# WKV stage: corner blocks of the chunk inverses made at once, one inverse product a step from the fifth step on, and a new order of the products behind it

## The chip, the cores and the metric

The kernel runs on one core of a Trainium2 chip (trn2). The metric is the device time of one execution in microseconds (us): median of 3 runs 2166.91, from 2166.88 to 2168.07. The profiler's execution has a span of 2162.8 us, 4.1 us less than that median; a number below is a number of that execution.

## The reference, cut to what matters

Two model blocks over 256 tokens of width 2048: attention, pooling and a gated feed-forward block, then an RWKV-7 mixer and a differential-attention mixer, all in fp32. The change lies in the mixer's recurrence:

```python
def step(S, inp):                       # 32 heads of 64 channels, 256 tokens
    r_t, w_t, k_t, v_t, kk_t, a_t = inp
    sa = jnp.einsum('bhvk,bhk->bhv', S, kk_t)
    S = (S * w_t[:, :, None, :]
         - sa[..., None] * (kk_t * a_t)[:, :, None, :]
         + v_t[..., None] * k_t[:, :, None, :])
    y = jnp.einsum('bhvk,bhk->bhv', S, r_t)
    return S, y
```

Behind it every head's output is normalised (group norm), scaled, a bonus term is added, it is gated by silu(g) and multiplied by `w_out`.

## The kernel before, in words

The heads are taken as 4 groups g of 8 heads, the tokens as 4 chunks c of 64 (`CHUNK`, `NCH`), which gives 16 steps n = 4g + c (`STEPS`). Inside a chunk the recurrence is solved by products of matrices: u = T x, where T is the inverse of a 64 x 64 unit-triangular matrix of each head and chunk. State S is carried from chunk to chunk of one group.

Ahead of the steps, beside 96 woven units of a projection, VectorE (DVE) inverts only the two 32 x 32 diagonal blocks of every T (`inverse_step`, L2983; `LT`, `TT`), 128 head-chunk pairs at once. They go to DRAM (`t_scratch`, L729) and come back step by step in the places that the products want (`load_t`, L665: four transfers of the diagonal blocks, two of the off-diagonal block `CRS` of the matrix itself). The corner of T is never made: a step multiplies by the diagonal blocks (u), by the corner of the matrix (w), adds w to x and multiplies by the diagonal blocks again.

One step on TensorE (PE; `step`, L1458) in program order, each product 8 calls of `quads` (L1313, one line L1319 for all) or 4 calls of a turn, and every fp32 call two matmul instructions in the trace: `x_second` (kappa by S), `k_pairs` of step n+1, first u product, `turn_v` of n+1, w product, (in the first step of a later group `group_squares` of the group before), `beta_pairs` of n+1, first part of y (r by S), second u product, `turn_k` of n+1, state product, `turn_beta` of n+1, `x_first` of n+1, second part of y. Turns of k and beta are left out where step n+1 is the last of its group (c = 3), the state product where n is.

Beside it ScalarE (ACT; `step`, L2231) copies x (L2234), the y of the step before (L2205), u (L2240), the turned v (L2210), half of the second u (L2246), the turned k and beta (L2216). DVE (`step`, L3051) masks the pairs (`read_kappa` L3037, `read_rho` L3043), adds w (L3057), copies the other half of the second u (L3063), adds to S and scales it (L3075, L3077). At some steps both do what belongs elsewhere: DVE a reciprocal at c = 0 of g = 1, 2, 3 (`head_reciprocal`), a `head_pair` at steps 7, 9, 11, 13, low halves of output weights (L2448) at steps 10, 14, 15, 15 (`LOW_SPLIT_AT`); ACT their high halves (L1692) at steps 6, 10, 14, 14 (`SPLIT_AT`). GpSimd (POOL) squares y (L866). SyncE (SP) issues every transfer, in program order, with its waits. Behind step 15 the output product starts as soon as the first four tiles of its operand are split (`operand_hi`, `operand_lo`, L2229, L3049).

The order is written by hand on every engine; no planner changes it.

## Time and profile before

| what | number |
|---|---|
| median of 3 runs | 2166.91 us |
| span of the profiled execution | 2162.8 us |
| PE busy | 2128.1 us (98%) |
| DVE, ACT busy | 1466.9, 1063.6 us (68%, 49%) |
| granted TensorE clock | full (2.4 GHz) in all 40 slices |
| instruction transfers (q8) | 88 of 1.44 MB in all, so 16 KB each |

A timeline row gives the start in us, the length, the engine, the line, the operation with what it writes and reads, and how many instructions are merged in it; a bracket is the engine's idle time before it and who ended it. PE's matmuls are pipelined, so the distance from one row's start to the next is what a product costs, not its length.

### The profile page before, as it was taken

The page shows a single profiled execution, that of the slowest core. Times are in us where ns is not written, and L with a number is a line of the kernel's source. Part 1 is how long each engine was busy: PE and PEld are TensorE (multiplying, and loading weights), DVE is VectorE, ACT ScalarE, POOL GpSimd, SP SyncE. Part 2 cuts the span into 40 slices and gives each one's busy share as a digit, 9 for nine tenths or more (in the row PEclk, how much of TensorE's full clock was granted, in tenths as well). Part 3 has the DMA queues.
Part 4 walks back from the last instruction along what each step waited for, and adds up shares of the span by engine and source line. Part 5 has one row for each costly group of instructions (what it writes and reads, how often), then busy time and mean ns, then how long its engine had stood idle before and what let it go on. Part 6 is the DMA issues. An engine that isn't in the chain of part 4 may idle for free.

```text
span 2162.8 us, 36139 instructions
## 1 busy us (share of the span) xinstructions
PE 2128.1 (98%) x13990; PEld 1808.1 (84%) x13990; DVE 1466.9 (68%) x2083; ACT 1063.6 (49%) x1516; POOL 85.8 (4%) x75
## 2 busy tenths in 40 slices
PE   9999999999999999999899999999899999999998
PEld 7888878888888888888788888887788888888886
DVE  6556568885478855786795599884776544567656
ACT  5444455444444433444644766544434534456543
POOL 0800000000000000000000000001211000000000
PEclk9999999999999999999999999999999999999999
DMA  9654545555656556555465656653454555654553
GB/s 299 202 165 157 172 160 185 190 186 189 198 185 190 187 187 199 187 180 177 150 203 167 196 183 179 206 160 86 129 174 142 185 185 195 186 155 146 173 197 117
DMA packets 398856, 384.43 MB, mean 178 GB/s; under 512 B 43660, under 2 KB 395460, under 8 KB 397764
## 3 DMA queue, kind: packets, MB, share of 16 engines
q1 hardware_dynamic: 398728, 382.66, 55.8%
q8 instruction: 88, 1.44, 0.3%
q14 instruction: 40, 0.33, 0.1%
HBM read 375.73 MB, written 6.87 MB: 177 GB/s over the span
## 4 chain that ended last, share of the span: by engine, by line
PE 89%; DVE 7%; issue 2%; ACT 1%; DMA 1%; POOL 0%; SPq 0%; DVEq 0%; ACTq 0%; POOLq 0%
PE acc L894 35%; PE acc L897 17%; PE acc L1020 5%; PE acc L1022 5%; PE acc L1021 5%; PE acc L931 3%; PE acc L986 2%; PE acc L987 2%; PE acc L988 2%; PE aux L1319 2%; PE acc L934 1%; DVE w_lo L3001 1%; PE acc L1619 1%; PE acc L1620 1%; PE acc L1621 1%
## 5 line engine op out<-in xcount | busy, mean ns | idle before, releaser
L2448 DVE TENSOR_TENSOR w_lo<-raw_w,w_hi 128x1024 fp32r<-128x1024 f32 (+1 forms) x570 | 683.5, 1224 | 438.3 <-ACT w_hi L1692 437.5
L1692 ACT ACTIVATE w_hi<-raw_w 128x1024 fp32r<-128x1024 f32 (+1 forms) x570 | 586.3, 1045 | 706.0 <-PE acc L897 413.0
L894 PE MATMUL acc<-h,w_hi 128*128 128x512 f32 x1664 | 525.8, 397 | 0.0
L897 PEld LDWEIGHTS acc<-h,w_lo 128*128 128x128 f32 x1664 | 312.6, 188 | 73.8
L897 PE MATMUL acc<-h,w_lo 128*128 128x256 f32 x1664 | 327.0, 278 | 0.0
L894 PEld LDWEIGHTS acc<-h,w_hi 128*128 128x128 f32 x1664 | 254.7, 189 | 1.0
L894 PE MATMUL acc<-x_split,w_hi 128*128 128x512 f32 x704 | 225.1, 401 | 0.0
L894 PE MATMUL acc<-xs_b,w_hi 128*128 128x512 f32 x512 | 162.0, 398 | 1.0 <-DVE w_lo L3001 0.9
L897 PEld LDWEIGHTS acc<-x_split,w_lo 128*128 128x128 f32 x704 | 132.2, 188 | 31.2
L3001 DVE TENSOR_TENSOR w_lo<-raw_w,w_hi 128x1024 fp32r<-128x1024 f32 x96 | 116.8, 1219 | 42.1 <-ACT w_hi L2165 41.2
L894 PE MATMUL acc<-xs_a,w_hi 128*128 128x512 f32 x448 | 142.3, 399 | 0.7 <-DVE w_lo L3001 0.7
L897 PE MATMUL acc<-x_split,w_lo 128*128 128x256 f32 x704 | 138.7, 278 | 0.0
L1020 PE MATMUL acc<-w_hi,ff 128*128 128x512 f32 x346 | 135.2, 391 | 2.9 <-DVE w_lo L2448 2.9
L1021 PE MATMUL acc<-w_lo,ff 128*128 128x512 f32 x352 | 137.5, 391 | 0.0
L1022 PE MATMUL acc<-w_hi,ff 128*128 128x512 f32 x346 | 135.1, 390 | 0.0
L2165 ACT ACTIVATE w_hi<-raw_w 128x1024 fp32r<-128x1024 f32 x96 | 100.8, 1054 | 53.2 <-PE acc L897 45.6
L897 PEld LDWEIGHTS acc<-xs_b,w_lo 128*128 128x128 f32 x512 | 96.2, 188 | 22.7
L894 PEld LDWEIGHTS acc<-x_split,w_hi 128*128 128x128 f32 x704 | 108.1, 189 | 2.4 <-issue 0.8
L897 PEld LDWEIGHTS acc<-xs_a,w_lo 128*128 128x128 f32 x448 | 84.2, 188 | 20.0
L897 PE MATMUL acc<-xs_b,w_lo 128*128 128x256 f32 x512 | 100.6, 278 | 0.0
L897 PE MATMUL acc<-xs_a,w_lo 128*128 128x256 f32 x448 | 88.1, 278 | 0.0
L894 PEld LDWEIGHTS acc<-xs_b,w_hi 128*128 128x128 f32 x512 | 78.0, 189 | 3.4 <-issue 1.6
(459 smaller groups left out, 3223.5 us busy)
## 6 DMA issues: line engine op xcount, KB each, us to landing
raw_w<-in_w_up SPq DMA_DIRECT2D x172, 512.0 KB, 3.5
raw_w<-in_a_w_in SPq DMA_DIRECT2D x124, 512.0 KB, 3.9
raw_w<-in_w_in SPq DMA_DIRECT2D x64, 512.0 KB, 3.9
raw_w<-in_w_down SPq DMA_DIRECT2D x64, 512.0 KB, 3.5
raw_w<-in_b_w_qg SPq DMA_DIRECT2D x64, 512.0 KB, 3.7
raw_w<-in_w_o SPq DMA_DIRECT2D x32, 512.0 KB, 3.5
raw_w<-in_a_w_out SPq DMA_DIRECT2D x32, 512.0 KB, 3.5
raw_w<-in_w_k_shared SPq DMA_DIRECT2D x32, 512.0 KB, 3.3
```

Of the source, the lines that this page charges most:

```text
L894: pe.matmul(ACC[2 * b + f], WHI[:, q if hi is None else hi, k, f * P:(f + 1) * P], op[:, kt, :, :].rearrange("p h t -> p (h t)"), start=fi ...
L897: mm = pe.matmul(ACC[2 * b + f][:, 0:T], WLO[:, slot, k, f * P:(f + 1) * P], op[:, kt, 0, :], start=False, stop=last)
L931: pe.matmul(ACC[2 * b + f], hi(2 * x + b)[:, k, f * P:(f + 1) * P], op[:, kt, :, :].rearrange("p h t -> p (h t)"), start=first, stop=False)
L986: pe.matmul(out, xh, wh[:, :, k, :], start=(kt == 0), stop=False)
L987: pe.matmul(out, xh, wl[:, :, k, :], start=False, stop=False)
L1020: pe.matmul(out[t_], xh, wh, start=(x + k == 0), stop=False)
L1021: pe.matmul(out[t_], xh, wl, start=False, stop=False)
L1022: mm = pe.matmul(out[t_], xl, wh, start=False, stop=(x == 3 and k == ku - 1))
L1692: act.activation(WHI[:, u % 4, 0:ku, :], RAWW[:, u, 0:ku, :], ACT.Copy).then_inc(hi_made, 1)
L2165: act.activation(WHI[:, n % 4, :, :], RAWW[:, slot, :, :], ACT.Copy).then_inc(hi_made, 1)
L2448: dve.tensor_tensor(WLO[:, u, 0:ku, :], RAWW[:, u, 0:ku, :], WHI[:, u % 4, 0:ku, :].bitcast(F32), ALU.subtract)\
L3001: dve.tensor_tensor(WLO[:, slot_of(n), :, :], RAWW[:, slot_of(n), :, :], WHI[:, n % 4, :, :].bitcast(F32), ALU.subtract)\
```

## The change

The corners of all T are now made once. TT's blocks are stored in whole 64 x 64 places of `t_scratch` whose corners are blanked first (`blank_corners`). ACT writes the first diagonal blocks turned (`left_turned`), they go out and come back by row (`LEFT_ALL`), the second diagonal blocks come back too (`RIGHT_ALL`), the matrices' corners are loaded at once (`CROSS_ALL`). PE makes corner products of 128 calls of 32 x 32 by 32 in step 0 and again in step 1; ACT and DVE copy their results, and SP stores the corners of groups 1 to 3. Steps 0 to 3 (`WHOLE` = 4) still use two u products and w. From step 4 on `whole_step` uses the whole T: one u product, and right behind it the state product; the turns of v, k and beta, `k_pairs` (now two steps ahead) and `x_first` follow. The first part of y stands ahead of u, the group's squares at the end of the step, y has one PSUM bank in turn, S two buffers. ACT and DVE follow that order; `read_kappa` looks two steps ahead and stands ahead of the reciprocal, the head pairs and the splits. `load_t` is one transfer from step 4 on. The bonus rows are spread behind the stored corners. The diff, without declarations of buffers and semaphores, and without lines taken away from functions printed above:

```diff
@@ -561,8 +569,32 @@
...
-STATE_SUMS = BANKS[:, 3, T:].rearrange("p (e x) -> p e x", e=2)
-XU_BANKS, Y_BANKS = SIDE[:, 0:2, :], SIDE[:, 2:4, :]
+GROUP_SUMS = BANKS[:, 3, T:]
+XU_BANKS, CORNER_BANKS = SIDE[:, 0:2, :], SIDE[:, 2:4, :]
+WHOLE = NCH
+CORNERS_IN, CORNERS_COPIED, ALL_STORED = 16 + 12 * 16, 2, 5 * 16
+def y_bank(n):
+    return SIDE[:, 2 + n % 2, 0:T].rearrange("p (e x) -> p e x", e=2)
+def state_sums(n):
+    return SIDE[:, 2 + (n + 1) % 2, T:].rearrange("p (e x) -> p e x", e=2)
+def s_after(n):
+    return (S, S_ODD)[n % NCH % 2]
+def u_count(n):
+    return n + 1 + min(n + 1, WHOLE)
+def us_count(n):
+    return 2 * (n + 1) + min(n + 1, WHOLE)
+def t_count(n):
+    return sum(16 if k >= WHOLE else 48 for k in range(n % 3, n + 1, 3))
@@ -665,14 +697,29 @@
 def load_t(n):
...
-    src = t_dram.rearrange("(f c h) b s t -> c h b s f t", c=NCH, h=2)
-    for hh in range(2):
-        for b in range(2):
-            at = 64 * hh + H * b
-            sp.dma_start(TB[at:at + H, m, :, H * b:H * b + H], src[c, hh, b, :, 4 * g:4 * g + 4, :])\
-              .then_inc(t_loaded[m], 16)
-    for e in range(2):
-        sp.dma_start(CRS[64 * (1 - e):64 * (1 - e) + H, m, :, H:], cross_dram[g, c, e]).then_inc(t_loaded[m], 16)
+    src = t_dram.rearrange("(g i c h) s t -> g c (h s) i t", g=4, c=NCH, h=2)
+    sp.dma_start(TB[:, m, :, :], src[g, c]).then_inc(t_loaded[m], 16)
+    if n < WHOLE:
+        for e in range(2):
+            sp.dma_start(CRS[64 * (1 - e):64 * (1 - e) + H, m, :, H:], cross_dram[g, c, e]).then_inc(t_loaded[m], 16)
+def blank_corners():
+    sp.wait_ge(blanked, 2)
+    for a, b in ((0, H), (H, 0)):
+        sp.dma_start(t_dram[:, a:a + H, b:b + H], TB[:, 0, 0:1, 0:H].broadcast_to([P, H, H])).then_inc(t_stored, 16)
+def load_left_and_right(g):
+    sp.dma_start(LEFT_ALL[H * g:H * g + H, :, :], left_dram[32 * g:32 * g + 32].rearrange("a r s -> r a s")).then_inc(inv_in, 16)
+    sp.dma_start(RIGHT_ALL[H * g:H * g + H, :, :], t_dram[32 * g:32 * g + 32, H:, H:].rearrange("a s t -> s a t")).then_inc(inv_in, 16)
+def store_corners():
+    sp.wait_ge(blanked, 2 + 2 * CORNERS_COPIED)
+    for g in range(1, 4):
+        sp.dma_start(t_dram[32 * g:32 * g + 32, 0:H, H:].rearrange("a s t -> s a t"), CORNERS[H * g:H * g + H, :, :])\
+          .then_inc(bon_stored, 16)
 def store_lt(f):
@@ -724,13 +771,22 @@
...
+    if n == 88:
+        blank_corners()
...
-sp.dma_start(t_dram, TT[:, :, :, :]).then_inc(t_stored, 16)
-sp.wait_ge(blanked, 2)
-sp.wait_ge(t_stored, 16)
-for n in range(3):
-    load_t(n)
+for b in range(2):
+    sp.dma_start(t_dram[:, H * b:H * b + H, H * b:H * b + H], TT[:, b, :, :]).then_inc(t_stored, 16)
+for g in range(4):
+    sp.dma_start(CROSS_ALL[H * g:H * g + H, :, :].rearrange("s (b x) t -> s b (x t)", x=4), cross_dram[g].rearrange("c e s x t -> s (c e) (x t)")).then_inc(inv_in, 16)
+sp.wait_ge(inverted, 2)
+sp.dma_start(left_dram, OUTER[:, :].rearrange("p (r s) -> p r s", r=H)).then_inc(t_stored, 16)
+sp.wait_ge(t_stored, ALL_STORED)
+load_t(0)
+for g in range(4):
+    load_left_and_right(g)
+load_t(1)
+load_t(2)
 def first_unit(n, w):
@@ -757,11 +813,15 @@
...
-for g in range(4):
-    spread_bonus(g)
...
+    if n == WHOLE:
+        sp.wait_ge(bon_stored, 64 + 48)
...
+    if n == WHOLE - 1:
+        store_corners()
+        for g in range(4):
+            spread_bonus(g)
@@ -1453,52 +1513,120 @@
     g, c = STEPS[n]
     pe.wait_ge(x_begun, 3 * g + c)
     pe.wait_ge(s_ready, 3 * g + c)
...
+    quads(XU_BANKS, 0, at(KAP, n), state(n), between, False, True).then_inc(x_done, 1)
+def u_product(n):
+    quads(XU_BANKS, P, block_of(TB[:, n % 3, :, :]), mid(XS), across, True, True).then_inc(u_done, 1)
+def state_product(n):
+    g, c = STEPS[n]
+    pe.wait_ge(us_ready, us_count(n))
+    if c < 3:
+        pe.wait_ge(kb_out, k_beta_turned(n))
+        pe.wait_ge(y_out, n)
+        quads(state_sums(n), 0, kb(n % 2), vu(n % 2), channel, True, True, one_bank=True).then_inc(s_done, 1)
+def y_first(n):
+    if n > 1:
+        pe.wait_ge(y_out, n - 1)
+    quads(y_bank(n), 0, state(n), at(R, n), channel, True, False, one_bank=True)
+def y_second(n):
+    pe.wait_ge(rest_out, n + 1)
+    if n > 1:
+        pe.wait_ge(y_out, n - 1)
+    quads(y_bank(n), 0, vu(n % 2), rho(n % 2), channel, n % NCH == 0, True, one_bank=True).then_inc(y_done, 1)
+def corner_products(lhs, rhs):
+    for a in range(H):
+        for g in range(4):
+            rows = slice(H * g, H * g + H)
+            mm = pe.matmul(CORNER_BANKS[rows, a // 16, a % 16 * H:a % 16 * H + H], lhs(a)[rows], rhs[rows, a, :], start=True, stop=True)
+    mm.then_inc(corner_done, 1)
+def cross_of(a):
+    i, c, hh = a // 8, a // 2 % 4, a % 2
+    return CROSS_ALL[:, 8 * c + i % 2 * 4 + 2 * (hh ^ i % 2) + i // 2, :]
+def corners_halfway():
+    pe.wait_ge(inv_in, CORNERS_IN)
+    pe.wait_ge(kb_out, 1)
+    corner_products(cross_of, LEFT_ALL)
+def corners():
+    pe.wait_ge(blanked, 2 + CORNERS_COPIED)
+    pe.wait_ge(y_out, 1)
+    corner_products(lambda a: HALFWAY[:, a, :], RIGHT_ALL)
 def step(n):
     g, c = STEPS[n]
...
+    state_next = STEPS[n + 1][1] < 3
+    if c > 0:
+        x_second(n)
+    k_pairs(n + 1)
+    pe.wait_ge(t_loaded[n % 3], t_count(n))
+    pe.wait_ge(xs_ready, n + 1)
+    u_product(n)
+    turn_v(n + 1)
+    pe.wait_ge(us_ready, us_count(n) - 2)
+    quads(XU_BANKS, T, far(CRS[:, n % 3, :, :]), far(US), between, True, True).then_inc(w_done, 1)
+    if n == 0:
+        corners_halfway()
+    if n == 1:
+        corners()
+    beta_pairs(n + 1)
+    if n > 1:
+        y_first(n)
+    pe.wait_ge(ws_ready, n + 1)
+    u_product(n)
+    if state_next:
+        turn_k(n + 1)
+    if n < 2:
+        pe.wait_ge(blanked, 2 + CORNERS_COPIED * (n + 1))
+    if n == 1:
+        y_first(n)
+    state_product(n)
+    if state_next:
+        turn_beta(n + 1)
+    if n + 1 < WHOLE:
+        x_first(n + 1)
+    y_second(n)
+    if n + 1 == WHOLE:
+        k_pairs(n + 2)
+        x_first(n + 1)
+def whole_step(n):
+    g, c = STEPS[n]
     more = n + 1 < len(STEPS)
     state_next = more and STEPS[n + 1][1] < 3
...
     if c > 0:
         x_second(n)
+        y_first(n)
     if more:
...
+        beta_pairs(n + 1)
+    pe.wait_ge(t_loaded[n % 3], t_count(n))
     pe.wait_ge(xs_ready, n + 1)
...
+    u_product(n)
+    state_product(n)
+    if c == 2:
+        pe.wait_ge(gn_read, g)
     if more:
         turn_v(n + 1)
...
+    y_second(n)
     if state_next:
         turn_k(n + 1)
...
     if state_next:
         turn_beta(n + 1)
...
+    if c == 0:
+        pe.wait_ge(vt_out, 2 * n + 4)
+        group_squares(g - 1)
+    if n + 2 < len(STEPS):
+        k_pairs(n + 2)
+    if more:
         x_first(n + 1)
...
 gates = [quarters(operand, per) for per in (1, 2, 2)]
 for n in range(NW):
@@ -2145,6 +2276,11 @@
 def pair_hi(s_, p):
...
+def left_turned():
+    act.wait_ge(inverted, 1)
+    act.activation(OUTER[:, :].rearrange("p (r s) -> p r s", r=H), TT[:, 0, :, :].rearrange("p s r -> p r s"), ACT.Copy).then_inc(inverted, 1)
 def woven_out(j0):
@@ -2202,7 +2340,12 @@
...
+    act.activation(y4, by_two(y_bank(n)), ACT.Copy).then_inc(y_out, 1)
+def corner_copy(n):
+    act.wait_ge(corner_done, n + 1)
+    act.activation((HALFWAY, CORNERS)[n][:, 0:H // 2, :], CORNER_BANKS[:, 0, :].rearrange("p (a t) -> p a t", a=H // 2), ACT.Copy).then_inc(blanked, 1)
 def v_copies(n):
@@ -2230,23 +2373,32 @@
 def step(n):
     g, c = STEPS[n]
+    more = n + 1 < len(STEPS)
     act.wait_ge(x_done, n + 1)
     act.activation(in_slots(XS), by_two(XU_BANKS[:, :, 0:P]), ACT.Copy).then_inc(xs_ready, 1)
...
+    if n < WHOLE:
+        if n:
+            y_copy(n - 1)
+        else:
+            woven_out(2)
+        act.wait_ge(u_done, u_count(n) - 1)
+        act.activation(in_slots(US), by_two(XU_BANKS[:, :, P:T]), ACT.Copy).then_inc(us_ready, 1)
         v_copies(n + 1)
...
+        if n < 2:
+            corner_copy(n)
+    act.wait_ge(u_done, u_count(n))
     act.activation(v_and_u(n % 2)[0:64, :, 1, :, :].rearrange("p j h t -> p h j t"), by_two(XU_BANKS[0:64, :, P:T]), ACT.Copy)\
        .then_inc(us_ready, 1)
...
+    if n >= WHOLE and more:
+        v_copies(n + 1)
+    elif n >= WHOLE:
+        operand_hi(0)
+    if n >= WHOLE and more:
+        y_copy(n)
+    if more:
         k_beta_copy(n + 1)
+    if n == WHOLE - 1:
+        y_copy(n)
     if n == 0:
         silu(7)
     if n == 2:
@@ -3051,15 +3203,14 @@
 def step(n):
     g, c = STEPS[n]
     more = n + 1 < len(STEPS)
...
+    if n < WHOLE:
         read_kappa(n + 1)
...
+        dve.wait_ge(w_done, n + 1)
+        dve.tensor_tensor(slots(XS), by_two(XU_BANKS[:, :, T:384]), slots(XS), ALU.add).then_inc(ws_ready, 1)
+    if n < 2:
+        dve.wait_ge(corner_done, n + 1)
+        dve.tensor_copy((HALFWAY, CORNERS)[n][:, H // 2:, :], CORNER_BANKS[:, 1, :].rearrange("p (a t) -> p a t", a=H // 2)).then_inc(blanked, 1)
+    dve.wait_ge(u_done, u_count(n))
     dve.tensor_copy(v_and_u(n % 2)[64:P, :, 0, :, :].rearrange("p j h t -> p h j t"), by_two(XU_BANKS[64:P, :, P:T])).then_inc(us_ready, 1)
     if more:
         read_rho(n + 1)
@@ -3068,28 +3219,29 @@
     if c < 3:
         decay = GCE[:, 4 * g:4 * g + 4, c].rearrange("p (j e) -> p e j", e=2).unsqueeze(3).broadcast_to([P, 2, 2, CHUNK])
+        s_new, ps = slots(s_after(n)), by_two(state_sums(n))
         dve.wait_ge(s_done, 3 * g + c + 1)
...
         if c > 0:
...
+            dve.tensor_tensor(s_new, ps, slots(s_after(n - 1)), ALU.add).then_inc(s_taken, 1)
+            dve.wait_ge(s_taken, 2 * g + c)
+            dve.tensor_tensor(s_new, s_new, decay, ALU.mult).then_inc(s_ready, 1)
         else:
...
+            dve.tensor_tensor(s_new, ps, decay, ALU.mult).then_inc(s_ready, 1)
+    pair = 2 * (g - 2) + 1 if c == 1 and g > 1 else 2 * (g - 1) if c == 3 and 0 < g < 3 else None
+    wide = [GWIDE[:, (2 if c == 1 else 0) + k, :] for k in range(2)]
+    if c == 0 and g:
+        dve.wait_ge(gn_sq_sum, g)
+        dve.tensor_scalar(GROWS[:, 0, :], GROUP_SUMS, 1.0 / CHUNK, GN_EPS, ALU.mult, ALU.add).then_inc(gn_read, 1)
+    if n + 1 >= WHOLE and n + 2 < len(STEPS):
+        read_kappa(n + 2)
     if c == 0 and g:
         head_reciprocal(g - 1)
...
     for u in heads_at(n, LOW_SPLIT_AT):
         split_unit(u)
...
+    if pair is not None:
+        if c == 3:
+            dve.wait_ge(gn_loaded, 32 * g)
+        head_pair(pair, wide)
 def head_reciprocal(g):
     dve.wait_ge(gn_read, g + 1)
```

## Rows read from the trace of the kernel before

**Rows 1.** Stretches: busy us and instructions by engine, clock, DMA share, GB/s.
```profile
1448.50:1458.40 9.90, 9.90 (x59) 8.63 (x57) 4.28 (x4) 3.32 (x5) 0.00 (x0) 1.00 0.18 28
1467.30:1563.90 96.60, 86.59 (x2666) 70.87 (x2665) 55.83 (x109) 48.41 (x117) 23.50 (x24) 1.00 0.34 90
```
**Rows 2.** Timeline, PE: second u product of step 3; the output product's first.
```profile
1488.59 0.46 PE L1319 MATMUL aux<-wkv_x,inverse_blocks 64*64 64x64 f32 x16
...
1563.88 0.74 PE L931 MATMUL acc<-wkv_out,w_hi 128*128 128x512 f32 x2 [0.57 <-DVE wkv_out L3049]
```
**Rows 3.** Timeline of PE alone, step 9, from turn_v to step 10's x.
```profile
1523.78 0.66 PE L1401 MATMUL acc<-consts,x 128*64 128x128 f32 x8
1524.37 0.46 PE L1319 MATMUL aux<-wkv_u,cross_blocks 64*64 64x64 f32 x16
1524.65 0.41 PE L1386 MATMUL acc<-r_kappa,beta 64*64 64x64 f32 x16
...
1525.38 0.46 PE L1319 MATMUL aux<-wkv_x,inverse_blocks 64*64 64x64 f32 x16
1525.77 0.66 PE L1407 MATMUL acc<-consts,k 128*64 128x128 f32 x8
1526.39 0.69 PE L1319 MATMUL acc<-wkv_small 128*64 128x64 f32 x16
1526.90 0.61 PE L1407 MATMUL acc<-consts,beta 128*64 128x128 f32 x8
1527.44 1.08 PE L1319 MATMUL aux<-wkv_small 64*64 64x64 f32 x32
1528.45 0.46 PE L1319 MATMUL aux<-wkv_s,r_kappa 64*64 64x64 f32 x16
```
**Rows 4.** Timeline of all engines, step 10's second u to step 11's first.
```profile
1531.49 0.46 PE L1319 MATMUL aux<-wkv_x,inverse_blocks 64*64 64x64 f32 x16
...
1532.02 0.43 DVE L3063 COPY wkv_small<-aux 64x256 f32<-64x256 f32 x1 [0.58 <-PE aux L1319]
...
1532.51 0.69 PE L1319 MATMUL acc<-wkv_small 128*64 128x64 f32 x16 [0.55 <-DVE wkv_small L3063]
...
1534.31 0.46 PE L1319 MATMUL aux<-wkv_s,r_kappa 64*64 64x64 f32 x16
1534.56 0.65 PE L1376 MATMUL acc<-r_kappa,k 64*64 64x128 f32 x16
...
1534.83 0.38 ACT L2234 ACTIVATE wkv_x<-aux 128x256 f32<-128x256 f32 x1 [1.48 <-PE aux L1319]
...
1535.28 0.42 DVE L3037 TENSOR_TENSOR wkv_small<-acc,consts 128x256 f32<-128x256 f32 x1
...
1535.36 0.46 PE L1319 MATMUL aux<-wkv_x,inverse_blocks 64*64 64x64 f32 x16
```
**Rows 5.** Timeline: side work of DVE and ACT, group squares on PE.
```profile
1527.92 0.87 DVE L3108 SCALAR_TENSOR_TENSOR beta<-beta,params,head_rstd_wide 128x256 f32<-128x256 f32 x2
...
1528.83 0.88 DVE L3113 SCALAR_TENSOR_TENSOR beta<-beta,params,bonus 128x256 f32<-128x256 f32 x2
...
1542.70 0.64 PE L1423 MATMUL aux<-group_norm_squares,consts 128*32 128x128 f32 x16 [0.79 <-POOL group_norm_squares L866]
...
1545.82 1.75 DVE L3096 RECIPROCAL head_rstd_rows<-head_rstd_rows 128x256 f32<-128x256 f32 x1
...
1556.55 1.99 ACT L1692 ACTIVATE w_hi<-raw_w 128x1024 fp32r<-128x1024 f32 x2
...
1562.60 1.23 DVE L3049 TENSOR_TENSOR wkv_out<-beta,wkv_out 128x1024 fp32r<-128x1024 f32 x1
```
**Rows 6.** Timeline of SP: the inverses' store and the first load back.
```profile
1442.55 0.34 SPq L729 DMA_DIRECT2D t_scratch<-inverse  x1
1448.43 1.76 SPq L672 DMA_DIRECT2D inverse_blocks<-t_scratch  x4
```
**Rows 7.** Timeline, step 5: a product broken in its middle.
```profile
1501.05 0.32 PEld L1319 LDWEIGHTS aux<-wkv_x,inverse_blocks 64*64 64x64 f32 x15 [0.91 <-issue]
```

More of the change, by code:

```diff
@@ L275, in program @@
                 with ExitStack() as s3:
+                    CORNERS = sb(s3, "corners", [P, CHUNK // 2, CHUNK // 2])
+                with ExitStack() as s3:
                     HTP = sb(s3, "xs_pair", [P, 2, T])
@@ L303, in program @@
                     LT, TT = (sb(s3, n, [P, 2, CHUNK // 2, CHUNK // 2]) for n in ("lt_blocks", "inverse"))
+                with ExitStack() as s3:
+                    CROSS_ALL, LEFT_ALL, RIGHT_ALL, HALFWAY = (sb(s3, n, [P, CHUNK // 2, CHUNK // 2])
+                                                               for n in ("cross_all", "left_all", "right_all", "corner_halfway"))
                 BON = sb(s2, "bonus", [P, KD, T])
@@ L1422, in group_squares @@
                     for i in range(4):
[L1423 removed]
+                        mm = pe.matmul(GROUP_SUMS[32 * i:32 * i + 32, e * P:(e + 1) * P], HEADSEL[:, 30:62], GSQ[:, i, e * P:(e + 1) * P], start=True, stop=True)
                 mm.then_inc(gn_sq_sum, 1)
```

90 lines of the change are left out of this document (16 added, 74 removed).

## The prediction

> **What bounds the kernel now.** I read the page first: TensorE is busy nearly all the span at full clock, so outside the changed stage nothing can move but through PE. Then the stretches [rows 1]: the sixteen steps last from about 1467.3 to 1563.9, and in these 96.6 us PE has 86.6 us in work, DVE 55.8 and ACT 48.4. So the stage is mostly a queue of small products on PE, with some waiting. Then the timeline of one step [rows 3] against one with a shorter queue [rows 4]: from one product's start to the next there is no hole in the first, while in the second PE stands 0.55 us in front of the state product, waiting for DVE's copy of u. That is what decides this change: in the old order a turn of k fills the time in which u is copied, in the new order the state product is directly behind u and nothing fills it.
>
> **Prices from these rows.** A 64x64 product whose four tiles work together (x's second term, w) costs 0.25 to 0.28; u about 0.39 with its entry [rows 3, 4]. The state product costs 0.51. x's first and y's second term together take 1.01 [rows 3]; x takes 0.25 and y is of the state product's kind, 0.51, so 0.25 is left for two changes of the tile shape, 0.12 each. Turn of beta 0.54, less one change 0.42; turn_v 0.59, less a change and its slower entry 0.43; turn of k taken as 0.43. k_pairs: its row is 0.65 long where x's row is 0.46 for a cost of 0.25, so 0.65 - 0.21 = 0.44 [rows 4]. Latencies [rows 4]: u's start to the state product's 1.02 (copy begins at 0.53); state product to the next x term at least 1.80; x term to u 1.05 (copy begins at 0.52); k_pairs to the mask of kappa 0.72, which lasts 0.42.
>
> **Whole steps (4 to 15).** Behind the start S of the state product PE now has: state 0.51, turn_v 0.43, y 0.51, turn_k 0.43, turn_beta 0.42, one change 0.12, k_pairs 0.44, x_first 0.25, in all 3.11. That is over the 1.80 that the state itself needs, so PE's queue sets it. Then x to u 1.05, which hides y's first term and beta_pairs (0.25 + 0.73 [rows 3] = 0.98), and u to S 1.02, of which 0.6 is bare. A step with c = 1 costs 3.11 + 1.05 + 1.02 = 5.18. c = 2 has no turns of k and beta, 5.18 - 0.85 = 4.33. c = 3 has no state product and x_first stands in x_second's place, 5.18 - 0.51 - 0.25 = 4.42. c = 0 has the group squares as well, whose row is like a turn's [rows 5], with a change on either side about 0.5: 5.68; the 0.79 that they waited for POOL goes, since the squares of the group before are then a whole step old.
> From step 3's second u product [rows 2] to step 4's u: 1.02 to us's arrival, turn_beta 0.42, y 0.51, change 0.12, k_pairs 0.44, x to u 1.05 = 3.56. Three c = 0 steps 17.04, three c = 1 15.54, two c = 2 8.66, two c = 3 8.84. Step 14: 1.02 + 1.80 + 1.05 = 3.87. Step 15 to the output product: ACT's copy ends at 0.91, only then comes its high half (1.0, half of the row of two in [rows 5], the same shape), then DVE's low half 1.23, so 3.3. Sum 60.8.
> **What the side work costs.** It was behind PE's queue and is now in front of a copy that PE waits for. The mask of kappa ends 1.14 behind k_pairs' start; the reciprocal adds 1.75, in all 2.89 [rows 5]. The next u copy is wanted at 0.44 + 0.25 + 1.05 + 0.53 = 2.27: 0.6 late, three times, 1.9. A head pair is 0.87 + 0.04 + 0.88 = 1.79: 0.66 late at steps 9 and 13, and at 7 and 11, where no x_second lies between, 0.91 late: 3.1. ACT's split (1.0) stands between y's copy, which ends about 3.3 behind u, and the next x copy, wanted at 3.8 in steps 6 and 10: 0.57 late twice, 1.1; in step 14 there are two, ready at 5.35 against 3.34: 2.0. Together 8.1, so 60.8 + 8.1 = 68.9. The old stretch is 1563.88 - 1488.59 = 75.3 [rows 2]. **Gain 6.4 us.** Its bounds: 8.1 more if none of the side work comes in the way, and 3 us less if each of the 12 steps keeps a change of tile shape and a longer entry of 0.25.
>
> **Steps 0 and 1: the corner products.** Nothing goes out of these steps, and each gets 128 calls, 256 matmuls. Neither 32x32 tiles nor 32 columns at this rate occur in the trace. Sixteen instructions of 64x64 by 64 take 0.25. If columns bound, half of it per sixteen: 16 x 0.125 = 2.0 us a product. If issue bounds, 16 x 0.25 = 4.0. There is a third price: loads and matmuls together are 512 instructions, while the whole stage issues 5331 in 96.6 us, 55 per us [rows 1]; in 2 us that would be 250 per us. That code arrives late even at the low rate is my reading of step 5, where one product stands 0.91 after its first weight load with "issue" as the cause, so with no semaphore to wait for [rows 7]; two such holes a product give 2.0 + 1.8 = 3.8, and with issue as bound 5.8. I take 3.4, nearer to the middle of the first two, because some code is already there, and keep 2.0 and 5.8. Behind the product DVE and ACT copy 512 columns before the copy of u; turn_k hides most in step 0 (0.1 left with the change of shape), and in step 1 turn_k and the moved y term do, at 0.1 to 0.3. Sum 2 x 3.4 + 0.2 = **7.0 us lost.**
>
> The page TensorEngine Tiling of the Trainium skill, under Gotcha 1: PSUM Pressure, speaks against this change: row tiles cannot use the same PSUM bank at once. The corner products do this with four. In [rows 3] two row tiles write each bank in other partitions (x's term) at four tiles' full rate, so the trace does not agree for two. As a mechanism, tiles taken one after another would make 16 instructions cost 4 x 0.125 = 0.5 and a product 8.0.
> TensorE: Matmul & The Clock Gate of the same skill, under Wait — 56ns, not 53.3ns?, gives about 25 ns as the least distance between matmul starts; 256 of them would be 6.4 us a product and the whole 2174.0 by that page, an estimate. The row has 16 in 0.25 us, 16 ns each [rows 4], so it does not hold across tiles here.
>
> **Transfers.** SP stored the inverses at 1442.55 and could load at 1448.43 [rows 6]. Now in that place: two stores of 4096 pieces of 128 bytes, four loads of corners, a wait for ACT's turned block (free at about 1448), its store. Between 1448.5 and 1458.4 eighteen loads with 128 pieces each took 0.18 of 16 engines [rows 1], 28.5 engine-us for 2304 pieces, 12.4 ns a piece: two stores are 6.3 us. Stored at about 1457.5, step 0's T in at about 1460, well before step 0 (1467.3). The eight loads of left and right blocks, 1024 pieces each, are 6.3 us more: in at about 1467.5 with their latency, wanted in front of the first corner product at about 1469.7. Hidden, with 2 us to spare; if that cover goes, each piece that takes twice as long costs up to 10 us. I put 0.5 us into the sum. The blanking, 6.3 us of DMA time beside weights, meets loads asked for some 7 units ahead. Later loads get shorter (one instead of six) and the bonus rows are spread later but needed only at step 7: nothing.
>
> **Sum.** -6.4 + 7.0 + 0.5 = +1.1: span 2163.9, and with the 4.1 us between this execution and the median **2168.0 us**.
>
> **Rivals.**
> 1. Faster. DVE's and ACT's side work fits into gaps (say half of the 8.1 is not felt) and columns bound the corner products: gain 10.4, cost 4.2, 2166.9 - 6.2 = 2160.7. For it: DVE is busy only 58% of the stage [rows 1]. Against it: the order on each engine is fixed, and the reciprocal stands right there.
> 2. Slower: step 0 waits for the left and right blocks. Price: if pieces of 128 bytes in long transfers need 18 instead of 12.4 ns, the stores end 3 us later and the loads another 3; less the 2 us of slack that is 4 us, and with code as the corner products' bound (3.8) one more: 2173. It decides from the point at which they land after 1469.7.
> 3. Slower still: the four tiles of a corner product work one after another (8.0 each): 2168.0 + 9.2 = 2177.
> 4. The corner products cost 2 us each and the rest is as forecast: 2165.2, within my forecast's own range.
>
> **Chances.** Forecast with its own range 2163 to 2172, 0.50 (rival 4 in it); faster 0.25; late loads or late code 0.20; serial tiles 0.05. This kernel's time can be told apart from no change at about 0.2%, 4.3 us: faster is below 2162.6, slower above 2171.2. Faster 0.25, within 0.49, slower 0.26. The range that leaves out two in ten reaches from 2160.5 (rival 1) to 2175 (most of rival 2).
>
> **What would show it.** Right: whole steps of 5.2, 4.3, 4.4 us and 5.7 for c = 0; a hole of about 0.6 us in front of every state product behind a u copy; the reciprocal, head pairs and splits followed by u or x copies that begin late; corner products of 2 to 4 us in steps 0 and 1; the output product 3.3 us behind the last u. Wrong: corner products over 5 us, or a wait for left_all or right_all in front of the first of them (rival 2 or 3); steps under 5 us at c = 0 and 1, with DVE free when u is ready (rival 1); PE holes with "issue" inside the corner products put the fault on code, not on tiles. The forecast is also wrong if weights of the woven units come late behind the blanking, which would show as PE waits around 1430 to 1445.

## The result, and the profile after

The changed kernel takes 2182.04 us (median of 4 runs, 2178.71 to 2187.66) against 2166.89 for the kernel before: ratio 1.0078, 95% interval 1.0061 to 1.0095. On a second chip it was 1.0073 (1.0056 to 1.0090). It is 15 us slower. The forecast was 2168.0 with a range from 2160.5 to 2175.0, so it was wrong by 14 us and outside its range.

The profiled execution took 2187.66 us (span 2186.1), the slowest of its four; its 23.3 us over the span before are placed first, and what is peculiar to it is named. These are the stretches of the changed kernel: steps 0 to 3 (from the first u product to step 3's second u product), the rest of the steps up to the output product's first matmul, the output product, and what follows. Columns: stretch and its length, busy us of PE, its weight loads, DVE, ACT and POOL with instructions, granted clock, DMA share, GB/s.

```profile
1466.18:1508.06 41.88, 29.46 (x1112) 24.88 (x1104) 10.86 (x22) 12.28 (x29) 1.84 (x3) 0.84 0.41 89
1508.06:1581.25 73.19, 56.86 (x1677) 50.31 (x1673) 43.08 (x77) 34.48 (x78) 22.82 (x21) 0.95 0.37 102
1581.25:1681.50 100.25, 98.56 (x583) 82.18 (x584) 69.46 (x78) 38.62 (x41) 7.59 (x5) 0.97 0.55 177
1681.50:2186.10 504.60, 495.69 (x2618) 421.08 (x2616) 296.78 (x380) 245.43 (x353) 5.43 (x4) 0.98 0.53 167
```

The same four stretches of the kernel before (cut at the same instructions; [rows 2] has two of the marks):

```profile
1467.80:1488.59 20.79, 18.65 (x600) 15.35 (x592) 9.47 (x20) 11.07 (x27) 1.84 (x3) 1.00 0.22 51
1488.59:1563.88 75.29, 67.42 (x2062) 55.01 (x2058) 46.34 (x89) 36.93 (x90) 21.64 (x21) 1.00 0.37 100
1563.88:1661.70 97.82, 95.95 (x583) 80.03 (x584) 69.43 (x78) 39.31 (x42) 8.73 (x5) 1.00 0.55 179
1661.70:2162.80 501.10, 494.14 (x2618) 419.73 (x2617) 296.64 (x380) 245.36 (x353) 5.44 (x4) 0.99 0.53 168
```

Line by line: steps 0 to 3 +21.1 us, steps 4 to 15 -2.1, output product +2.4, the rest +3.5, and the first u product begins 1.6 earlier (in the profiled runs below it begins anywhere from 1462.6 to 1468.9, except where calls are added ahead of it, so that is no effect of the change). Sum 23.3. In the last two stretches PE has the same number of instructions and less clock. The corner products of step 0, on PE (start, length, operation, what it stood idle for):

```profile
1467.92 0.46 PE L1379 MATMUL aux<-wkv_u,cross_blocks 64*64 64x64 f32 x16
1468.32 1.30 PE L1546 MATMUL aux<-left_all,cross_all 32*32 32x32 f32 x130
1471.37 1.27 PE L1546 MATMUL aux<-left_all,cross_all 32*32 32x32 f32 x126 [1.75 <-issue]
1472.57 0.32 PE L1446 MATMUL acc<-r_kappa,beta 64*64 64x64 f32 x2
1475.11 0.59 PE L1446 MATMUL acc<-r_kappa,beta 64*64 64x64 f32 x11 [2.21 <-issue]
```

The 256 matmuls run at 10 ns each, 2.57 us together, in two bursts, and behind each burst PE waits for nothing that has a semaphore. Between the two waits lie 126 + 2 = 128 matmuls with a weight load each: 256 instructions. In step 1 the same calls stand around waits of 1.1 and 2.5 us, again 128 matmuls apart. The waits of PE in steps 0 to 3 (engine and line, what ended the wait; us in total, times, longest):

```profile
PE aux L1546 <- issue: 5.3, 3, 2.5
PE aux L1379 <- issue: 3.1, 1, 3.1
PE acc L1446 <- issue: 2.2, 1, 2.2
PE acc L1461 <- DVE silu_g L2678: 0.7, 1, 0.7
PE aux L1379 <- DVE wkv_small L3214: 0.6, 1, 0.6
```

Issue waits are 10.6 us, the calls themselves 5.1. At a granted clock of 0.84, 13.4 of the 41.9 us ran at 1.2 GHz and not 2.4 (0.16 x 2 x 41.9). Of the 21.1 us by which these steps grew, 5.4 are left for that. One of its spells:

```profile
1474.40:1481.20 6.80, 6.09 (x114) 5.41 (x118) 1.54 (x3) 1.49 (x3) 0.00 (x0) 0.50 0.01 2
```

The 3.1 us wait stands in step 3's w product, far from any corner product; SP had just issued the spread of the bonus rows (SP's queue, then PE):

```profile
1492.70 5.56 SPq L800 DMA_DIRECT2D bonus<-bonus_scratch  x8
```

```profile
1507.08 0.40 PE L1379 MATMUL aux<-wkv_u,cross_blocks 64*64 64x64 f32 x12 [3.08 <-issue]
```

In step 9 DVE's head pair, whose first two instructions take 0.87 us in [rows 5], took long, while POOL multiplied the bonus rows. DVE's and POOL's timelines:

```profile
1545.84 2.57 DVE L3260 SCALAR_TENSOR_TENSOR beta<-beta,params,head_rstd_wide 128x256 f32<-128x256 f32 x2
```

```profile
1545.38 2.36 POOL L909 TENSOR_TENSOR bonus<-bonus,x 128x1024 f32<-128x1024 f32 x1
```

One of the two took 2.18 us and the other 0.47.

The trace also has the transfers that bring instructions (queue q8, 16384 bytes each). Each of the five issue waits in steps 0 to 3 ends shortly behind one of them:

| wait, us | it ends at | q8's transfer | wait's end behind it |
|---|---|---|---|
| 1.75 | 1471.37 | 1468.98 to 1470.07 | 1.30 |
| 2.21 | 1475.11 | 1472.48 to 1473.63 | 1.48 |
| 1.08 | 1485.30 | 1482.92 to 1483.88 | 1.42 |
| 2.46 | 1489.04 | 1486.46 to 1487.68 | 1.36 |
| 3.08 | 1507.08 | 1504.30 to 1505.55 | 1.53 |

The same holds for every issue wait of 0.8 us or more from 1455 to 1590 us in all seventeen profiled runs (55 waits): it ends 1.2 to 1.7 us behind a transfer that took 0.9 to 1.5 us. So these are waits for instructions.

What was feared did not come: with the blanking's transfers PE's stretch ahead of the steps is full at full clock, and no wait for the left and right blocks stands ahead of the corner product.

```profile
1430.00:1466.00 36.00, 36.00 (x271) 30.90 (x274) 20.98 (x30) 14.85 (x19) 0.00 (x0) 1.00 0.89 198
```

### The profile page after: what moved, and what is told of

Its sections match the earlier page's. It is cut to its first block, busy times and chain, and to the rows that moved or that the text cites. A ratio compares the mean times of both kernels' runs of the same rounds, so it can differ in the third digit from the quotient of the medians.

```text
span 2186.1 us, 36327 instructions
## 1 busy us (share of the span) xinstructions
PE 2131.7 (98%) x14118; PEld 1815.8 (83%) x14118; DVE 1465.4 (67%) x2073; ACT 1063.7 (49%) x1507; POOL 85.9 (4%) x75
## 4 chain that ended last, share of the span: by engine, by line
PE 90%; DVE 7%; issue 2%; ACT 1%; POOL 0%; DVEq 0%; ACTq 0%; POOLq 0%
PE acc L954 35%; PE acc L957 17%; PE acc L1080 5%; PE acc L1082 5%; PE acc L1081 5%; PE acc L991 3%; PE acc L1046 2%; PE acc L1047 2%; PE acc L1048 2%; PE acc L994 2%; PE aux L1379 2%; DVE w_lo L3153 1%; PE acc L1750 1%; PE acc L1751 1%; PE acc L1752 1%
```

## The experiments

Theory ("code"): TensorE's instructions come in pieces of 256. While small products run at 100 matmuls (200 instructions) per us, the next piece is not there yet, and each piece costs a wait of 1.3 to 2.7 us (1.1 to 2.7 in all runs); half clock follows the waits. Rivals: the small tiles or their columns are dear in themselves; the new order of the steps is the loss. Ratios are to the kernel before on the same chip.

**The same calls in the kernel before.**

```diff
+                if n < 2:
+                    for a in range(32):
+                        for q in range(4):
+                            rows = slice(32 * q, 32 * q + 32)
+                            pe.matmul(Y_BANKS[rows, 0, P:P + 32], IDENT[rows, 32 * q:32 * q + 32], CENTRE[rows, 0:32], start=True, stop=True)
                 if more:
                     beta_pairs(n + 1)
```

> The kernel before with 128 calls of 32 rows by 32 columns added in step 0 and in step 1, behind w, whose sums nobody reads; nothing is left out. Code theory: the same holes at every 256th instruction as in the changed kernel, 1.3 to 2.7 us each, and half clock behind some: 2167 + 9 to + 15 = 2176 to 2182. Rival (the calls cost only their columns, and the loss is in the new order): 2 x 2.0 to 2.5, so 2171 to 2172.

Measured: 2178.00 us, ratio 1.0071 (1.0054 to 1.0088), +14.2 us.

```profile
1462.64:1500.25 37.61, 27.96 (x1113) 24.16 (x1105) 9.48 (x20) 11.07 (x27) 1.84 (x3) 0.82 0.14 32
1500.25:1574.48 74.23, 67.63 (x2062) 55.21 (x2057) 46.38 (x89) 36.93 (x90) 21.62 (x21) 1.00 0.38 101
```

```profile
1464.77 1.30 PE L1481 MATMUL aux<-consts 32*32 32x32 f32 x130
1467.54 1.26 PE L1481 MATMUL aux<-consts 32*32 32x32 f32 x126 [1.46 <-issue]
1468.73 0.33 PE L1386 MATMUL acc<-r_kappa,beta 64*64 64x64 f32 x2
1471.55 0.59 PE L1386 MATMUL acc<-r_kappa,beta 64*64 64x64 f32 x12 [2.50 <-issue]
```

Without one transfer, copy or reordering of the change, steps 0 to 3 grow from 20.8 to 37.6 us, and the waits stand at the same places, 126 + 2 matmuls apart. Steps 4 to 15 give 1.1 us back. The time was inside the expected 2176 to 2182, and the whole loss can come from these calls. The DMA share there is 0.14, so no traffic is needed for it.

**A quarter of the columns.** The same edit with `P:P + 8` and `CENTRE[rows, 0:8]`.

> The kernel before with the 128 calls in step 0 and in step 1 again, now with 8 columns each in place of 32: the same number of instructions, a quarter of the columns. Nothing is left out. Code theory: the holes stay, 1.6 to 2.7 us at every 256th instruction; +11 to +15 over the kernel before. Rival (columns): +4 at most. The run with 32 columns was +14.

Measured: 2179.96 us, ratio 1.0071 (1.0055 to 1.0088), the same as with 32 columns.

```profile
1466.85 1.26 PE L1481 MATMUL aux<-consts 32*32 32x8 f32 x130
1469.81 1.22 PE L1481 MATMUL aux<-consts 32*32 32x8 f32 x126 [1.70 <-issue]
1470.96 0.32 PE L1386 MATMUL acc<-r_kappa,beta 64*64 64x64 f32 x2
1473.27 0.59 PE L1386 MATMUL acc<-r_kappa,beta 64*64 64x64 f32 x12 [1.99 <-issue]
```

Even the bursts last as long: columns cost nothing here, instructions do. The rival of columns falls.

In the seven profiled runs with all 128 calls together, the second wait of each product ends 3.46 to 4.01 us behind the first, 256 instructions later. That is the pace at which code came: the next transfer began 1.0 us or more after a wait's end, took about 1.1, and the wait ended about 1.4 behind it. A burst that uses up a piece in 1.3 us waits for the rest.

**The same calls beside wide matmuls.** The 256 calls of 32 columns, 32 behind each of eight units of the woven products (units 84 to 91).

> The kernel before with the same 256 calls (32 rows, 32 columns), but 32 behind each of eight units of the woven products, at about 1410 to 1445, where wide matmuls leave time for the code to come. Nothing is left out. Code theory: no holes, only their issue at 10 ns each: +5 to +6.5 us. Rival (the calls are dear wherever they stand): +14.

Measured: 2170.88 us, ratio 1.0027 (1.0016 to 1.0038), +5.7 us. The groups stand from 1431.7 to 1458.1, 3.67 us apart. The stretch that holds nearly all of them; the kernel before has x185 matmuls in the same stretch:

```profile
1430.00:1460.00 30.00, 30.00 (x645) 25.76 (x644) 19.52 (x28) 10.50 (x12) 0.00 (x0) 1.00 0.39 122
```

No wait of any kind and full clock. PE took 1289 instructions in these 30 us, 43 per us, under the 64 to 74 per us of the pace above; the expected 5 to 6.5 us came. So small calls are dear only where the instructions around them are short too.

**In portions.** The same 256 calls in eight portions of 32, two in each of steps 0 to 3 (ahead of y's first term and ahead of turn_k).

> The kernel before with the same 256 calls (32 rows, 32 columns) in eight portions of 32, two in each of steps 0 to 3. Nothing is left out. If the pace of the code decides (a piece of 256 instructions every 3.5 to 3.7 us, as the steps with corner products show): steps 0 to 3 have 2512 instructions, 9.8 pieces, 34 to 36 us against 20.8, so +13 to +15, or +10 if no half clock comes with it. Rival (only closeness is dear, and portions are hidden as beside the wide matmuls): +5 to +6.

Measured: 2174.97 us, ratio 1.0055 (1.0038 to 1.0071), +11.3 us. That lies between the two numbers for the pace (10 without half clock, 13 to 15 with it) and well over the rival's 5 to 6.

```profile
1464.60:1495.96 31.36, 25.47 (x1053) 21.74 (x1048) 9.48 (x20) 11.07 (x27) 1.84 (x3) 0.95 0.15 35
```

```profile
PE acc L1462 <- issue: 2.4, 2, 1.7
PE aux L1319 <- issue: 1.8, 2, 1.3
...
PE aux L1462 <- issue: 0.3, 1, 0.3
```

Seven of the eight portions lie in this stretch; the last stands behind the second u product of step 3. It grew by 10.6 us, of them 4.5 the calls and 4.5 issue waits. With steps 4 to 15 (76.4 us) that is 11.7 us, against 15.8 with the calls in two blocks: portions save some 4 us and hide little of the rest. The forecast's 2512 instructions were a wrong count: the stretch has 2101 (x1053 matmuls and x1048 loads), 8.2 pieces, 3.8 us a piece, within the 3.46 to 4.01 above. Without the calls it is 4.5 us a piece (x600 and x592 in 20.8 us) and there is no wait: these steps stood close to that pace already.

**The changed kernel with fewer instructions.** First 2 calls of 128 rows and 512 columns for each corner product, then 32 calls of 128 rows and 32 columns. Both leave out the correct corner blocks; all else is as it is. The first edit:

```diff
-                        rows = slice(H * g, H * g + H)
-                        mm = pe.matmul(CORNER_BANKS[rows, a // 16, a % 16 * H:a % 16 * H + H], lhs(a)[rows], rhs[rows, a, :], start=True, stop=True)
+                wide = (HALFWAY if rhs is RIGHT_ALL else CROSS_ALL).rearrange("p (a b) t -> p a (b t)", b=4)
+                for b in range(2):
+                    mm = pe.matmul(CORNER_BANKS[:, b, :], wide[:, b, :], rhs[:, 16 * b:16 * b + 16, :].rearrange("p a t -> p (a t)"), start=True, stop=True)
```

> The changed kernel with each corner product as 2 calls of 128 rows and 512 columns: eight instructions a product, about the same columns per bank, everything else as it is. The corner blocks and the output are wrong. Code theory: the four holes (8.3 us), the issue of the calls (some 4.4 us) and the half-clock spells (2 to 5 us) go, about 1 us of columns stays: 2182 - 14 to - 17 = 2165 to 2168. Rival (the new order of the steps is the loss, steps 0 to 3 included): not under 2176. My recorded forecast without its corner term would give 2161 to 2162.

> The changed kernel with each corner product as 32 calls of all 128 rows in place of 128 calls of 32 rows: the same columns go through, with a quarter of the instructions. The blocks beside the diagonal are left in, so the corner blocks and the output are wrong. Code theory (TensorE waits for its instructions, which come in pieces of 256): 768 instructions less are three pieces less; the holes of 1.94, 2.43, 1.27 and 2.65 us shrink to one at most, and the spells at half clock behind them with them: 2182 - 7 to - 12 = 2170 to 2175. Rival (columns or the tiles themselves are slow): the same time as the changed kernel, 2180 to 2182. Rival (the new order of the steps is the loss): also 2180 to 2182.

Measured: 2170.98 us, ratio 1.0034 (1.0022 to 1.0047) with 2 calls; 2191.10 us, ratio 1.0122 (1.0098 to 1.0147) with 32 (three runs; a fourth took 7012.71 us, unexplained). The first:

```profile
1464.10:1488.64 24.54, 22.64 (x608) 16.82 (x600) 10.86 (x22) 12.28 (x29) 1.84 (x3) 1.00 0.53 110
1488.64:1565.55 76.91, 56.64 (x1679) 49.90 (x1675) 43.08 (x77) 34.36 (x78) 22.85 (x21) 0.95 0.43 113
```

```profile
1466.24 1.98 PE L1545 MATMUL aux<-left_all,cross_all 128*128 128x512 f32 x4
...
1495.09 0.28 PE L1379 MATMUL aux<-wkv_small 64*64 64x64 f32 x4 [3.57 <-issue]
```

Steps 0 to 3 last 24.5 us: 3.8 over the kernel before. Each wide product takes 1.9 us and makes its step 1.6 longer (from first to second u product 4.33 us for 2.75, and 3.56 for 1.99), which is 3.2. So the new order itself costs these steps 0.6 us, and as the cause of the loss there that rival falls. But the whole is 3 to 6 us over what I expected: a wait of 3.6 for a piece of code still stands behind the bonus spread, which makes steps 4 to 15 76.9 us long. The 32-call kernel missed by 20 us, for a reason of its own:

```profile
1467.80 12.23 PEld L1545 LDWEIGHTS aux<-left_all,cross_all 128*128 128x128 f32 x64
```

Each call now loads 128 columns of weights for 32 columns of data, 191 ns a load, so packing four blocks on a diagonal is no way out. The clock was 0.57 there, and 0.50 from 1471 to 1480, with PE busy all the time and no wait. So waits are not needed for half clock: how much of it in the changed kernel goes back to them, and how much to the small calls themselves, is not shown. The Trainium skill states (TensorE: Matmul & The Clock Gate, "LDWEIGHTS (loading the stationary operand)") that a load's time goes by its columns, not by its rows. The trace of the kernel before agrees: loads of 64 columns took 134 ns with 64 rows and 136 with 128, loads of 128 columns 188 ns with 97 rows and with 128.

**Three groups of corner blocks.** Steps 0 to 3 never read the blocks of group 0, so `range(4)` became `range(1, 4)`.

> The changed kernel with the corner blocks of groups 1 to 3 alone (96 calls a product, not 128): steps 0 to 3 use the old corner path, so those of group 0 are never read. Nothing that is needed is left out. Code theory: 256 instructions less are one piece of code and one hole of about 2.4 us less and 1.3 us less of issue, with less half clock: 3 to 5 us under the changed kernel. Columns alone (rival): 1.3 us under it.

Beside it ran the changed kernel again:

> The changed kernel as it is, for a time on the same chip as the runs beside it: 1.007 to 1.009 of the kernel before.

Measured: 2177.74 us against 2181.41, ratios 1.0056 (1.0040 to 1.0073) and 1.0073 (1.0056 to 1.0090): 3.7 us less, of which 1.3 is issue, as the code theory expected (3 to 5 us). The two intervals overlap; the stretch tells more: steps 0 to 3 took 35.15 us in place of 40.17.

**The bonus spread later.** Two broadcasts each in steps 4 to 7, GpSimd's products at steps 5, 7, 9, 11.

> The changed kernel with the spread of the bonus rows (eight broadcasts) taken from step 3 and given as two each to steps 4 to 7, with GpSimd's product of them two steps later. Nothing is left out. Code theory: the hole of 3.3 us in step 3's w product was a piece of code that stood behind the spread; it shrinks to 0 to 1 us, with some 1 us of half clock behind it: 2182 - 3 to - 4.5 = 2177.5 to 2179. Moving GpSimd's product also moves its collision with VectorE's head pair in step 9 (2.18 us for an instruction of 0.48). Rival (that hole is only the pace at which code comes after the corner products): within 1 us of 2182.

Measured: 2179.81 us, ratio 1.0075 (1.0058 to 1.0091).

```profile
1464.88:1502.94 38.06, 28.61 (x1113) 24.20 (x1105) 10.85 (x22) 12.27 (x29) 1.84 (x3) 0.82 0.29 65
1502.94:1576.41 73.47, 56.46 (x1678) 49.43 (x1674) 43.08 (x77) 34.20 (x78) 22.36 (x21) 0.96 0.44 120
```

The wait in step 3 shrank from 3.1 (and 2.3 in the second run of the changed kernel) to 0.4 us, as expected, and steps 0 to 3 took 38.1 us where the changed kernel has 40.2 and 41.9. But issue waits of 1.6 and 0.3 us came in steps 4 to 15, where there had been 0.8. Of 2 to 4 us hardly any reached the end: the ratio is that of the changed kernel (1.0073 to 1.0078), as the rival had it. That the spread lengthened the wait is shown for the wait, not for the whole time. In the changed kernel the transfer that ended this wait took only 1.25 us, but began 7.9 us behind the one before it, while the spread kept the DMA engines busy: it came late and was not slow.

**GpSimd's product out of the head pair's way.**

```diff
-                if n in (3, 5, 7, 9):
-                    times_v((n - 3) // 2)
+                if n in (3, 5, 7, 8):
+                    times_v((3, 5, 7, 8).index(n))
```

> The changed kernel with one edit: GpSimd's last product of the bonus rows stands at step 8 in place of step 9. Collision theory: the first instruction of VectorE's head pair in step 9 takes 0.48 us and not 2.18, the hole of 2.79 us in front of step 10's state product falls to 1.1, step 10 to 11 takes 6.2 us and not 7.95, and 1.7 to 2.4 us are won: ratio 1.0062 to 1.0068 where the changed kernel has 1.0073 to 1.0078. Rival (the instruction is slow by itself there): no change.

Measured: 2177.67 us, ratio 1.0066 (1.0050 to 1.0081). DVE's pair in step 9, then the stretch of steps 4 to 15:

```profile
1543.46 0.87 DVE L3260 SCALAR_TENSOR_TENSOR beta<-beta,params,head_rstd_wide 128x256 f32<-128x256 f32 x2
```

```profile
1507.35:1577.73 70.38, 55.38 (x1677) 48.70 (x1674) 41.69 (x77) 34.20 (x78) 22.79 (x21) 0.97 0.39 109
```

The ratio came where expected, though its interval overlaps that of the changed kernel. The plain sign is the step: 10 to 11 went from 7.95 (7.97 in the second run) to 5.06 us. The stretch fell from 72.9 and 73.2 to 70.4, but other steps differ by up to 1.4 us between the runs, with the half clock in them.

The Trainium skill states a reason (SBUF — State Buffer, "SBUF: two separate sides"): GpSimd and a VectorE instruction with two SBUF inputs share one pair of ports under an exclusive lock, held for the whole instruction, and the other blocks. The trace agrees: the pair's slow instruction lay under GpSimd's 2.36 us, and in the same 2.36 us DVE's mask of kappa, which reads PSUM, took its usual 0.42.

**The new order by itself, and the best whole version.** Both with the spread over steps 4 to 7 and GpSimd's products at steps 5, 6, 8, 10; the first with the 2-call corner products, so it leaves out the correct corner blocks; the second with the three groups of the run above, and leaves out nothing.

> Corner products as 2 wide calls each (corner blocks and output wrong), the bonus spread given as two broadcasts each to steps 4 to 7, and GpSimd's products of it at steps 5, 6, 8, 10, where no head pair of VectorE stands. What is left of the change is the new order of the steps. By the theory the 3.78 us hole of the two-call kernel shrinks and the collision with GpSimd (1.7 us) goes: its ratio of 1.0034 comes down by 4 to 5.5 us, to 1.0009 to 1.0016. By my forecast of the whole steps, 68.9 us from step 3's second u to the output product, against 75.3 before. Rival (the whole steps are no gain at all): ratio stays over 1.002.

> Everything is computed that is needed: corner blocks of groups 1 to 3 alone, the spread over steps 4 to 7, GpSimd's products at steps 5, 6, 8, 10. The kernel with three groups alone was 1.0056; less 1.7 for the collision and 1 to 3 for the spread: 1.003 to 1.0045 of the kernel before, so still slower, since three of the four holes of the corner products stay.

Measured: 2167.44 us, ratio 1.0017 (1.0008 to 1.0027), and 2172.58 us, ratio 1.0048 (1.0032 to 1.0063). Both are just above what was expected. The first can't be told from its rival (over 1.002) by the ratio, and its steps 4 to 15 won about half of the forecast. Its stretches:

```profile
1463.44:1487.99 24.55, 22.64 (x608) 16.82 (x601) 10.86 (x22) 12.26 (x29) 1.84 (x3) 1.00 0.39 87
1487.99:1559.77 71.78, 55.66 (x1678) 47.90 (x1674) 41.69 (x77) 34.27 (x78) 23.63 (x21) 0.99 0.48 128
1559.77:1659.65 99.88, 98.18 (x583) 81.84 (x584) 69.45 (x78) 38.65 (x42) 7.59 (x5) 0.98 0.55 176
```

Steps 4 to 15 won 3.5 us here (5.2 in the other), and still it is 3.7 us over the kernel before: 3.8 from steps 0 to 3, and 2.1 in the output product with 1.6 behind it. As 3.2 of the 3.8 are the wide stand-in products, the new order by itself comes out about even: what it wins in the steps it loses behind them. So the 15 us of the changed kernel are about what its corner calls cost (14.2 us in the kernel before). From the output product's first matmul to the end eight profiled runs with the new order need 602.4 to 602.6 us and two more 604.5 and 604.8; the six with the old order need 598.9 to 600.5. The output product itself takes 99.6 to 100.4 us in all ten (the mended kernel with filling, below, is an eleventh, with 97.8 and 601.4), 97.8 to 97.9 in all six, and it begins with a spell of half clock, here in the changed kernel:

```profile
1580.20:1587.00 6.80, 5.74 (x18) 4.88 (x19) 6.76 (x9) 0.89 (x1) 1.64 (x2) 0.50 0.65 272
```

**Filling the idle time.** One matmul of 256 columns more between u and the state product of each of steps 4 to 15, in the changed kernel and in the mended one.

> The changed kernel with one matmul more in each of steps 4 to 15, of 128 rows and 256 columns, between u and the state product, where TensorE waits 0.54 us or more for the copy of u; nobody reads its sums. Nothing is left out. Clock theory (the half clock at the start of the output product follows from the idle time in the new steps): the spell goes, the output product falls from 100.3 to about 97.9 us and with it 2.4 to 3.6 us of the whole, less up to 1 us for the added work: ratio 1.0055 to 1.0068 where the changed kernel has 1.0073 to 1.0078. Rival (the spell has another cause): the same time or up to 1 us more.

> The kernel with everything mended (three groups, spread over steps 4 to 7, GpSimd's products moved; ratio 1.0048) with the same twelve matmuls more. Clock theory: 2.4 to 3.6 us less, ratio 1.0030 to 1.0040. Rival: 1.0048 or a little over. In neither case is it faster than the kernel before.

Measured: ratio 1.0079 (1.0062 to 1.0095) and 1.0045 (1.0028 to 1.0062), so no gain in either. Their output products, in this order:

```profile
1579.56:1679.74 100.18, 98.47 (x583) 82.14 (x584) 69.49 (x78) 38.62 (x41) 7.58 (x5) 0.97 0.55 181
```

```profile
1571.04:1668.87 97.83, 96.01 (x583) 80.02 (x584) 69.39 (x78) 38.49 (x41) 7.58 (x5) 1.00 0.56 184
```

In the mended kernel the spell left the output product, 1.9 us, but the steps paid for the added work (72.8 us for 70.1); in the changed kernel it stayed, though its steps 4 to 15 took about 71 us and not 72.9 or 73.2. Both times lie with the rival. One profiled run of each can't settle it: PE's idle time in front may have a part in the spell, and its cause stays open.

**The squares first, in the kernel before.** At steps 7 and 11 GpSimd squares y before it multiplies by the gate.

> The kernel before with one edit: at steps 7 and 11 GpSimd squares y before it multiplies by the gate (1.27 us), and not behind it. TensorE waits 0.77 and 0.79 us for those squares in steps 8 and 12 (the squares of group g-1). If the order on GpSimd is the cause, both waits go: 1.0 to 1.6 us faster, ratio 0.9993 to 0.9995, at the edge of what can be measured; rival: VectorE's pair, moved by nothing, still ends late and the time is the same.

Measured: 2163.50 us, ratio 0.9996 (0.9987 to 1.0005). PE's two waits for the squares (1.6 us in all in the kernel before) are gone from its list. But its issue waits there rose from 0.9 to 2.1 us, and steps 4 to 15 took 75.6 us for 75.3, so nothing was won in them. The time can't be told from no change. None of the versions with the new order beats the kernel before.

## Why the prediction was wrong

**What bounds the kernel.** Right for the steps, and wrong in one sentence: "outside the changed stage nothing can move but through PE" was taken to mean that nothing moves. PE's clock moved there: about 3 us in the usual run (602.5 from the output product to the end, the middle of the profiled runs with the new order, against 599.4 with the old), 5.9 in the profiled one. No term of the sum held it. The table of the kernel before calls the clock full in all 40 slices; a slice shows only that it was 0.9 or more. Its mean was 0.994, so some 26 us of that run were at half clock, and 61 us of the changed kernel's (0.986).

**Steps 0 and 1, the failed step.** The term was 7.0 us with bounds 4.2 and 11.8. The same calls cost 16.8 us in the steps of the kernel before. The parts: issue 2.57 us a product, between my bounds. Code: I took two holes of 0.91 us a product from [rows 7] and, with 3.4 us a product, let even these count only in part, "because some code is already there"; there are two a product, but of 1.1 to 2.7 us. The one hole of the old trace was the end of a wait that had mostly been covered: it showed that the mechanism exists, not its price. The runs show the price as a pace, 3.46 to 4.01 us for 256 instructions. The half clock (13.4 us of it) was in no term. And I stopped at the sum of 5.8 without following the code to the next step: the pieces stay late through step 3, where the moved bonus spread added 2 to 3 us to a wait. I had put that move at nothing.

The Trainium skill has a page that I did not weigh: Advanced Engine Details and Errata, "ISA Cache", gives a cache line of 16 KB, 256 instructions. The waits 256 instructions apart and q8's transfers of 16384 bytes agree with it. What a piece costs comes from the runs alone. The pieces in [rows 1] could have been counted: 5331 instructions in 96.6 us are one piece per 4.6 us. With 1024 more in the first four steps there are some 2200, one per 2.4 us if those steps were to last 20.8 us, and nothing in the rows showed code coming that fast.

**Whole steps.** The forecast for steps 4 to 15 was 68.9 us; measured 73.2, then 70.4 without the collision, and 70.05 in the mended kernel. By steps, from u product to u product in the profiled run (side work put where it delays a copy):

| from u to u | forecast | measured |
|---|---|---|
| 3 to 4 | 3.56 | 4.97 (clock 0.5 for 3.4 us) |
| 4 to 5 | 5.68 | 6.01 |
| 5 to 6, 9 to 10, 13 to 14 | 5.18 + 0.6 | 5.73, 5.73, 5.72 |
| 6 to 7 | 4.90 | 4.73 |
| 7 to 8 | 4.42 | 4.69 |
| 8 to 9 | 6.59 | 6.89 |
| 10 to 11 | 5.56 | 7.95 (the collision) |
| 11 to 12 | 4.42 | 5.52 (an issue wait of 0.8) |
| 12 to 13 | 6.59 | 6.02 |
| 14 to 15 | 6.53 | 6.01 |
| 15 to output | 3.3 | 3.22 |

Ten of the thirteen are within 0.6 us. The hole in front of the state product is 0.54, as forecast 0.55, and the output product's wait behind the last u is as worked out:

```profile
1579.03 0.69 PE L1379 MATMUL aux<-wkv_small 128*64 128x64 f32 x16 [0.54 <-DVE wkv_small L3214]
...
1581.26 1.22 PE L991 MATMUL acc<-wkv_out,w_hi 128*128 128x512 f32 x2 [1.54 <-DVE wkv_out L3201]
```

The 4.3 us by which the steps missed are the collision (2.4 with the half clock behind it), the spell in step 3 (1.4) and code (1.1), less 0.6 by which the head pairs and splits were priced too high. The price of a moved instruction was right by itself; that GpSimd's 2.36 us would lie over it was not looked at.

**Transfers.** Right: hidden. Pieces of 128 bytes kept pace and the blocks were there before they were wanted; the blanking did not delay PE.

**Rivals.** 1: the side work was felt nearly as priced, so no. 2: named "late code" together with late loads at 2173; the loads were on time, and code was late by far more than that. 3: serial tiles, wrong: 10 ns a matmul with four row tiles in one bank, each on its own partitions; the rule that the prediction cites from the Trainium skill (TensorEngine Tiling, "Gotcha 1: PSUM Pressure") is not borne out here. 4: columns bind, wrong by the narrow calls. The range missed because its upper bound was built on one visible hole.

## What to carry to other kernels

Before adding small products to a stretch that is already made of small products, count instructions per us there: in these steps each 256 more cost 4 us (16.8 us for 1024), of which only 1.3 is their issue, while beside wide matmuls they cost 1.4. The steps of the kernel before ran at 57 instructions per us without a wait, and code came at 64 to 74 per us. Look behind a changed stage too: the new order won 3.5 us in its steps and some 3 us came back at half clock in the next stage, for a reason that the runs leave open. When side work or a GpSimd product moves, lay the two engines' rows over each other for SBUF operands.
